# Transposes of an eight-stage transformer block moved from TensorE to DMA from SBUF

## The reference

```
h = RMSNorm(x, g_mix)                                   # x: (8, 4096, 1024) float32
[B_c | C_c | V_c | Q | K | V_a | gate_c | gate_a] = h @ w_in      # 3x512, 3x512, 2x1024 columns
y_c = (B_c * causal_dwconv3(C_c * V_c)) @ w_conv_out
q, k = rope(RMSNorm(Q per 64)), rope(RMSNorm(K per 64))   # 4 heads, two sub-heads of 64 each
w   = softmax(q1 k1^T / 8) - lam * softmax(q2 k2^T / 8)   # causal by chunks of 64
y_a = (RMSNorm(w @ V_a per head, sub_norm) * 0.8) @ w_attn_out    # sub_norm: 128 values, one per column of a head
x = x + (sigmoid(gate_c) * y_c + sigmoid(gate_a) * y_a) @ w_o
h2 = RMSNorm(x, g_ffn)
x = x + (silu(h2 @ w_gate) * (h2 @ w_up)) @ w_down        # 2816 hidden columns
```

## Time and profile before

| | |
|---|---|
| median of 2 runs | 2315.78 us |
| the profiled execution | 2310.52 us |
| its span on the slowest core | 2308.9 us (others from 2303.4) |
| granted TensorE clock, mean of the span | 0.989 |
| busy: PE, VectorE, ScalarE, GpSimd | 2206.9, 967.6, 1004.5, 390.7 us |
| DMA written, share of 16 engines' time: SyncE's queue | 284.17 MB, 36.5% |
| the same: GpSimd's queue | 52.96 MB, 14.9% |

### The profile page before, as it was taken

The page is one execution under the profiler, slowest core; times in us unless marked ns, Lnnn a source line. Parts: engine busy times, 40 slices in busy tenths (PEclk is TensorE's granted clock), DMA queues, the critical chain, the costliest instruction groups (busy, mean ns, idle before and its releaser), DMA issues.

```text
span 2308.9 us, 40719 instructions; the slowest of 8 cores (2303.4 to 2308.9 us)
## 1 busy us (share of the span) xinstructions
PE 2206.9 (96%) x15488; PEld 1233.5 (53%) x15488; DVE 967.6 (42%) x1851; ACT 1004.5 (44%) x1558; POOL 390.7 (17%) x496
## 2 busy tenths in 40 slices
PE   5799997999999999999999999999999999999899
PEld 2344473445644475444754447545466455575347
DVE  5665415633465324643245332364323542312532
ACT  3353314433444425544355543555545565545210
POOL 4651113410132001400024000131001310001000
PEclk9899998999999999999999999999999999999999
DMA  9589999898733335333353333533325323235334
GB/s 217 118 135 158 184 190 262 186 242 192 236 137 113 128 129 210 121 128 124 134 192 112 119 109 113 200 106 106 116 91 205 128 83 107 91 113 166 119 122 144
DMA packets 94653, 339.75 MB, mean 147 GB/s; under 512 B 10496, under 2 KB 11392, under 8 KB 94336
## 3 DMA queue, kind: packets, MB, share of 16 engines
q1 hardware_dynamic: 79632, 284.17, 36.5%
q0 software_dynamic: 14832, 52.96, 14.9%
HBM read 340.24 MB, written 49.81 MB: 169 GB/s over the span
## 4 chain that ended last, share of the span: by engine, by line
PE 87%; DMA 5%; DVE 3%; ACT 2%; issue 1%; POOL 1%; SPq 0%; DVEq 0%; ACTq 0%; POOLq 0%
PE psB L913 27%; PE psB L784 15%; PE psB L940 13%; PE psO L700 10%; PE psB L586 6%; PE psB L678 6%; PE psB L887 5%; PE psB L855 5%; DMA xt<-x 2%; DMA wring<-wblk 1%; DMA wsc<-wring 1%; PE psB L534 1%; ACT Pb L683 1%; DMA out<-xt 1%; PE psB L636 1%
## 5 line engine op out<-in xcount | busy, mean ns | idle before, releaser
L683 ACT ACTIVATE Pb<-psB 128x1024 bf16<-128x1024 f32 (+1 forms) x576 | 527.5, 950 | 470.2 <-PE psB L678 456.8
L913 PE MATMUL psB<-h,wring 128*128 128x512 bf16 x2816 | 636.7, 380 | 12.5 <-DVE ep L722 6.9
L913 PEld LDWEIGHTS psB<-h,wring 128*128 128x128 bf16 x2816 | 263.7, 98 | 351.4 <-issue 56.5
L784 PE MATMUL psB<-h,wring 128*128 128x512 bf16 x1792 | 419.4, 382 | 9.1 <-ACT Pb L683 5.7
L940 PE MATMUL psB<-wring,big 128*128 128x256 bf16 x2816 | 319.3, 273 | 2.1 <-DVE big L925 1.9
L940 PEld LDWEIGHTS psB<-wring,big 128*128 128x128 bf16 x2816 | 270.0, 98 | 54.1 <-issue 23.7
L700 PEld LDWEIGHTS psO<-Vs,Pb 128*128 128x128 bf16 x4224 | 263.8, 98 | 54.2 <-issue 6.5
L700 PE MATMUL psO<-Vs,Pb 128*128 128x129 bf16 x4224 | 290.6, 221 | 1.7 <-ACT Pb L683 1.7
L784 PEld LDWEIGHTS psB<-h,wring 128*128 128x128 bf16 x1792 | 168.3, 98 | 220.8 <-issue 39.1
L921 DVE SCALAR_TENSOR_TENSOR scr<-scr,psB 128x512 f32<-128x512 f32 x176 | 121.1, 688 | 326.3 <-ACT scr L919 321.7
L919 ACT ACTIVATE scr<-psB 128x512 f32<-128x512 f32 x176 | 105.1, 597 | 283.3 <-PE psB L913 279.7
(11 more groups left out here) (87 smaller groups left out, 1589.7 us busy)
## 6 DMA issues: line engine op xcount, KB each, us to landing
wring<-wsc SPq DMA_DIRECT2D x363, 512.0 KB, 4.0
wring<-wblk POOLq DMA_DIRECT2D x95, 512.0 KB, 11.1
xt<-x SPq DMA_DIRECT2D x64, 512.0 KB, 6.9
wsc<-wring SPq DMA_DIRECT2D x58, 512.0 KB, 9.5
out<-xt SPq DMA_DIRECT2D x32, 512.0 KB, 4.3
wring<-wsc SPq DMA_DIRECT2D x24, 384.0 KB, 3.3
wring<-wblk POOLq DMA_DIRECT2D x8, 384.0 KB, 7.1
wsc<-wring SPq DMA_DIRECT2D x4, 384.0 KB, 4.6
```

The source lines that it names most:

```text
L683: act(act_ns(2 * N), lambda S1=S1, P=P, N=N: A.activation(out=Pb[:, P.slot, :, 0:N], in_=psB[:, S1.slot:S1.slot + 2, 0:N], func=AF.Exp, sc ...
L784: subs.append((lambda kc=kc: PEE.matmul(bank(B), lhsT=wring[:, W.slot, :].rearrange("p (k c) -> p k c", k=8)[:, kc, col * 128:(col + 1) * ...
L913: subs.append((lambda kc=kc, gu=gu, B=B: PEE.matmul(bank(B), lhsT=wring[:, W.slot, :].rearrange("p (k c) -> p k c", k=8)[:, kc, gu * 128:( ...
```

## The change

All 896 block transposes leave TensorE. In their place SyncE issues 160 transposing DMAs from SBUF to SBUF (`turn`): 64 of a 128x1024 tile for the norms, 64 of a 128x512 tile for q and k, 32 for the attention outputs. The PSUM banks that they used, the VectorE eviction L538 and the ScalarE copies L640, L644 and L753 go too. The norm's gain is now applied ahead of the transpose, where it is one value per column: a tile `gb_sb` holds both gains on all partitions (1 MB, loaded once), and L530 becomes an operation with two tensor inputs. The factor 0.8 sub_norm goes into the rows of w_attn_out: VectorE scales blocks 19 and 22 in the ring after each load from the float32 original, twice each. To make room, the ring has 7 slots for 8, `xn` 3 for 4 and `yq` 5 for 6. The planner assumes 1500 ns of SyncE for each transposing DMA, and twice its bytes.

```diff
-NBANK, NSLOT, NXT, NXN, NYQ, NP, NSCR, SCW, NSM, NST8 = 5, 8, 4, 4, 6, 4, 7, 514, 12, 4
+NBANK, NSLOT, NXT, NXN, NYQ, NP, NSCR, SCW, NSM, NST8 = 5, 7, 4, 3, 5, 4, 7, 514, 12, 4
...
+        gb = sb("gb_sb", [128, 2, D], F32)
...
+        def turn(fn, reads, writes, nbytes, pos, chan):
+            t = pl.add("sp", 1500.0, [(fn, reads, writes)], pos, dma=2 * nbytes)
+            t.chan = chan
...
+        dma(lambda: nc.sync.dma_start(out=gb[:], in_=gb_d), [], [C("gb")], 1048576, -105000.0, lambda: "gb")
...
+                if b in HB_AO:
+                    dve(750.0, lambda: V.tensor_scalar(out=wring[:, v.slot, :], in0=wring[:, v.slot, :],
+                                                       scalar1=cons[:, SN08:SN08 + 1], scalar2=None, op0=ALU.mult),
+                        [(v, 0), C("sn08")], [(v, 0)], pos)
...
-        def norm(X, t, dst, gcol0, pos):
-            XN, SM, B = val("xn"), val("sm"), val("bank")
+        def norm(X, t, dst, g, pos):
+            XN, SM = val("xn"), val("sm")
...
-            dve(780.0, lambda: V.tensor_scalar(out=xn[:, XN.slot, :], in0=xt[:, X.slot, :], scalar1=sm[:, SM.slot, 1:2],
-                                               scalar2=None, op0=ALU.mult), [(X, 0), (SM, 1)], [(XN, 0)], pos)
-            subs = []
-            for kc in range(8):
-                subs.append((lambda kc=kc: PEE.transpose(
-                    bank(B).bitcast(BF16).rearrange("p (c k) -> p c k", c=8)[:, kc, :],
-                    xn[:, XN.slot, kc * 128:(kc + 1) * 128], ident[:]), [(XN, 0), C("ident")], [(B, 0)]))
-            pl.add("pe", 8 * TR, subs, pos, kind="normT")
-            dve(1240.0, lambda: V.tensor_tensor(
-                out=h8[:, dst.slot, :, t * 128:(t + 1) * 128], in0=bank(B).bitcast(BF16).rearrange("p (c k) -> p c k", c=8),
-                in1=cst[:, gcol0:gcol0 + 8].unsqueeze(2).to_broadcast([128, 8, 128]), op=ALU.mult),
-                [(B, 0), C("cst")], [(dst, t)], pos)
+            dve(dve_ns(1024, True), lambda: V.scalar_tensor_tensor(
+                out=xn[:, XN.slot, :], in0=xt[:, X.slot, :], scalar=sm[:, SM.slot, 1:2], in1=gb[:, g, :],
+                op0=ALU.mult, op1=ALU.mult), [(X, 0), (SM, 1), C("gb")], [(XN, 0)], pos)
+            turn(lambda: nc.sync.dma_start_transpose(out=h8[:, dst.slot, :, t * 128:(t + 1) * 128], in_=xn[:, XN.slot, :]),
+                 [(XN, 0)], [(dst, t)], 262144, pos, lambda: ("xT", dst.slot, t))
...
-            pl.add("pe", 4 * TR, subs, pos, kind="qkT")
             if qk == 0:
-                act(act_ns(512), lambda: A.copy(out=qT[:, QT[j].slot, :, t * 128:(t + 1) * 128], in_=half()),
-                    [(B2, 0)], [(QT[j], t)], pos)
+                turn(lambda: nc.sync.dma_start_transpose(out=qT[:, QT[j].slot, :, t * 128:(t + 1) * 128], in_=yq[:, yv.slot, :]),
+                     [(yv, 0)], [(QT[j], t)], 131072, pos, lambda: ("qT", QT[j].slot, t))
...
-                pl.add("pe", 4 * TR, subs, at, kind="oT")
-                act(act_ns(512) + 90.0, lambda: A.activation(out=onT[:, h, :], in_=bank(B2).bitcast(BF16)[:, 0:512],
-                                                             func=AF.Copy, scale=cons[:, SN08:SN08 + 1]),
-                    [(B2, 0), C("sn08")], [(ON[j][h], 0)], at)
+                turn(lambda: nc.sync.dma_start_transpose(
+                    out=onT[:, h, :].rearrange("p (q c) -> p q c", q=4), in_=yq[:, yv.slot, :]),
+                    [(yv, 0)], [(ON[j][h], 0)], 131072, at, lambda: ("oT", h))
```

32 lines of the change are left out of this document (9 added, 23 removed).

## The result

The changed kernel takes 2390.6 us (2386.0 to 2395.2, two runs) against 2315.8: 1.032 times as long, 95% interval 1.023 to 1.041. It is slower, by 75 us. The profiled execution has a span of 2384.5 us, 75.6 more than before.

What follows compares the result with a forecast made beforehand. TensorE, busy 2206.9 of 2308.9 us, was taken as the bound. 54 us off and 39 on made 15 us faster than 2315.8, rounded to 2300; the range was 2268 to 2460, the forecast's own 2270 to 2345.

Steps and rivals of the forecast that it cites:

- What leaves: TensorE's stream: 896 transposes of 55 ns gone, 49 us, plus 5 us of waiting in line for q and k.
- Landing: One transposing DMA, issue to landing: 5 us in late stages, 10 us in stages 0 and 1.
- Start: First convolution: gains and the fourth transpose come late, so it begins 13 us later (bounds 8 and 30).
- Norms of stages 0 and 1: Norm to feed-forward in stages 0 and 1: 5 us more waiting each, 10 in all (0 to 25).
- Queries, keys and outputs: Transposes of q, k and attention outputs: consumers stand further on, so no waiting was added for them.
- Stages 2 to 6 and the last: Norm to feed-forward: 3 us for stages 2 to 6 together, 3 us for the last stage's uncovered transposes.
- w_attn_out on VectorE: VectorE waits for four float32 blocks to land, with PSUM evictions behind: 4 us (0 to 20).
- SyncE and the ring: Seven ring slots and weight loads behind transposes that wait on SyncE: 6 us lost (0 to 60).
- Rival 1: Transposing DMAs move 256-byte pieces at 169 ns each, 10.8 us per norm tile; 2451 us, chance 0.22.
- Rival 2: In stages 0 and 1, transposes stand on SyncE behind write-backs that wait: 72 us, time 2372, chance 0.20.
- Rival 3: TensorE's waits go as well, 25 us, and early transposes land in 5 us; 2265 us, chance 0.13.
- Rival 4: TensorE's stream is replaced one for one by waiting at consumers; 2316 us, chance inside the forecast's 0.45.

Runs made afterwards that it cites:

- late_only: Changed kernel with DMA transposes only for queries, keys, first norms from stage 3 and second norms, outputs from stage 2; gains loaded later; 1.006 of the kernel before.
- late_qko8: Kernel before, all pools as there, with only queries and keys from stage 3 and attention outputs from stage 2 turned by DMA; 0.994 of the kernel before.
- h0_pe: Changed kernel with the four mixing norms of stage 0 turned on TensorE, all other transposes by DMA; 1.029 of the kernel before.
- gain_late: Changed kernel with gains loaded in two halves, the second only after the first norm's transposes have landed; 1.033 of the kernel before.
- norms_only: Changed kernel with only the norms' 64 tiles turned by DMA, queries, keys and attention outputs on TensorE; 1.027 of the kernel before.
- qk_o_only: Changed kernel with only the 96 tiles of queries, keys and attention outputs turned by DMA, norms on TensorE; 1.012 of the kernel before.
- wb_pool: Changed kernel with the write-backs of the bfloat16 weight blocks issued from GpSimd's queue in place of SyncE's; 1.043 of the kernel before.

## Why the prediction was wrong

The forecast was 2300, the measurement 2391. It lies inside the stated range, but in the band given to "slower", and the forecast said faster. Of the 90 us between them some 60 fell in stages 0 and 1 (an estimate: at most 21 us off and 33 on were forecast there, so 12 on, and 72 came) and some 30 in the later ones. Two steps failed: the early transposes were priced far too low, those of queries, keys and outputs at nothing, and the stream time of the late ones was taken as saved. Step by step:

- **What leaves: 49 + 5 us.** The stream time per block was right: 27 us for 514 blocks in late_only, all 14 us in late_qko8. Wrong was to take it as shortening the kernel; of the 49, 24 came back as busy time of the other matmuls, half of it in stages 0 and 1, where the granted clock fell. The sign "busy time falls by some 80 us" was wrong on its own terms: it counted the overlapping drains that the prediction had just set aside, and 25 us were measured.
- **Landing: 5 us late, 10 us early.** Late it is better, 3.4 and 2.5 us. Early it was undersized: 8 to 14 us in median for norms, queries and outputs of stage 1 (keys 4.1), up to 21. And one term was missing altogether: that an issue can hold SyncE for 7 to 12 us when the rings are full, with the next transposes behind it. The rows I went by the earlier trace rows give landings of other transfers and no time of issue.
- **Start: 13 us.** The first convolution came at 56.8, 20 us late in place of 13. h0_pe gave back some 8, so as a term of the sum it was sized too high rather than too low. The gains did come at 30 and the fourth transpose went out at 42 and landed at 53, near what I had worked out, but gain_late showed that without the gains ahead the start is no earlier.
- **Norms of stages 0 and 1: 10 us.** This is the step that failed most. norms_only, which holds the norms of all stages and the start, lost 48 us net, 76 with its 28 us of stream. TensorE's own wait for h at the feed-forward part was 3.7 and 4.6 us, less than the 5 to 8 forecast; the loss sits in the chain ahead of it. I priced each norm by itself against the work that covers it; in the chain the delays add: block 15, issues 12 and 7, landing 7, for one norm.
- **Queries, keys and outputs: nothing.** The prediction let their consumers "stand further on" and gave them no price. qk_o_only lost 14 us net, 35 with its 21 us of stream, and the chain of stage 0 runs through the landing of a key tile (15.1 us) and of an output (13.8).
- **Stages 2 to 6 and the last: 3 + 3 us.** Right as far as the norm itself goes: the feed-forward part's three waits for h, 15.9 us, fall in stages 0, 1 and 7, none between, and the last stage's is 7.6 us, against 5.1 before. But the claim on which I staked the forecast, late stages shorter by 30 us, failed: from the second feed-forward part on it is 1844.7 us against 1841.5.
- **w_attn_out on VectorE: 4 us.** In the changed kernel VectorE waited 0.9 us for the four blocks in all: nothing. That hangs on the order, for in norms_only it waited 14.8 us.
- **SyncE and the ring: 6 us.** Undersized: the pools alone cost 14 us, and loads behind waiting transposes ate some 10 of the late gain. I had reckoned 25 us from use to use of a slot against a 4.0 us load, and gave the 11.1 us loads of the float32 phase no price of their own.

**The rivals.** Rival 1, small pieces: the mechanism is there (245 bytes a packet), the price was five times too high, 34 ns in place of 169; a norm tile is some 1,070 packets, 2.2 us of 16 engines, not 10.8. By the Trainium skill, "VectorE: DVE Perf Modes", "The three transpose paths", a block by DMA is 1309 ns; here four more blocks in one DMA cost 3.4 - 2.5 = 0.9 us, 0.23 each. The measurement decides. Rival 2, the queue's order, had the nearest time, 2372, and its rows are on the chain. wb_pool took the write-backs off SyncE and the time grew, but it put the wait on GpSimd ahead of the norms, so it doesn't refute this rival; it shows that long issues and landings remain without it. How the loss divides between the order and the full rings stays open. Rival 3 is refuted: the waits that went were replaced by more. Rival 4, one for one, is close to what late_only did over the late stages: 27 us less of busy time, 21 more of standing still.

Open: how much of the norms' early loss is issue, how much landing and how much the order on SyncE; and why late norms by DMA are worth less than queries, keys and outputs. A kernel with fewer float32 blocks in flight while transposes run was not tried.

## What to carry to other kernels

An operation moved from the bottleneck engine to DMA needs room in the rings at the place where it goes: here it paid 14 of 14 us for queries, keys and outputs after the float32 phase, nothing that could be shown for norms there, and cost several times that inside the phase. Look at the DMA share per slice before placing it, and decide by stage. Count what the move takes besides time, smaller pools here (0.6%), and what stands behind it on the issuing queue. And when an average shows room, ask in which stage it was taken.
